# Weaving Fourier products into the inverses of a gated delta rule

## The chip, the cores and the metric

One core of a Trainium2 chip runs the whole program. The metric is the device time of one execution, in microseconds (us).

## The reference

Two model blocks follow each other on a sequence of 512 tokens of width 1024. The first has two layers with four kinds of attention and a gated feed-forward. The second, the tail here, adds a context of 256 tokens and mixes positions in two ways: a Fourier mix over four groups of 128 channels, and a gated delta rule in both directions over chunks of 64 tokens with four heads. Then come an output projection and a convolutional feed-forward.

```
def fourier_mix(u, w_f):
    ug = u.reshape(bsz, length, F_GROUPS, F_DIM)
    y = jnp.fft.fft2(ug, axes=(1, 3), norm='ortho').real
    return jnp.einsum('blgc,gcd->blgd', y, w_f)

def gated_delta_chunked(q, k, v, beta, g, s0):
    ...
    a_mat = jnp.where(strict, jnp.einsum('nbhid,nbhjd->nbhij', kb, kc) * decay, 0.0)
    t_inv = lax.linalg.triangular_solve(eye + a_mat, ...)
    u_val, w_key = t_inv @ vb, t_inv @ (kb * jnp.exp(gc)[..., None])
    ...
    def step(s, xs):
        v_new = u_i - w_i @ s
        o_i = qd_i @ s + a_i @ v_new
        s = s * jnp.exp(gl_i)[..., None, None] + kd_i^T @ v_new
        return s, o_i

y = concat(fourier_mix(u), rmsnorm(o_forward + o_backward) * silu(z)) @ w_out
```

## The kernel before

**Dense products.** A planner (`Dense`) writes out all projections as blocks in order and gives each output one of four PSUM banks (dense 0 and 1, scores 0 and 1) and each weight item its place in the stream. SP loads item n into raw slot n mod 4, once the last reader of item n - 4 has marked itself on `dense_mark`; GpSimd (POOL) loads the same item in rounded form into one of three high slots and subtracts the two (L2870), so TensorE (PE) runs three passes per block (L840 to L842).

**The tail up to the scan.** PE first computes the projections qkv, u and z. Then come two products that fold the Fourier weights into a cosine and a sine matrix (L1255). For each of the four Fourier groups follow eight channel products of 128 x 128 (L1264), whose result ScalarE (ACT) copies to p1 and p2, and eight position products of 128 x 512 (L1271) with a 2 MB position matrix, which accumulate in one bank and which ACT copies (L1867). The position matrix has a place of its own (`DFT_AT`); SP loads it in four loads (L820) during qkv. After the Fourier groups PE transposes v (L1283), makes the six row matrices of the decays (L1295, L1296) in dense 0 and 1, transposes k (L1303, L1311), and computes the token products of keys and queries (`token_products`, L1327).

**The inverses.** The twelve chunks are taken in three groups; each has both directions (d = 0, 1) of two token blocks. A triangular inverse is built in levels 1 to 5. In a level PE makes z from the masked matrix (`level_z`, L1354), ACT copies it (L1899), PE makes the update (`level_update`, L1366), and VectorE (DVE) subtracts it (L2643) and transposes (L2646), which the next level's z waits for. POOL makes each level's mask (L3044). In group 0 DVE also makes the other groups' matrices in each level (`make_a`, `make_x`, L2606 to L2627), and PE transposes four of them after levels 4 and 5 (`turn_x`, L1339). At the end of a group `w_and_u` forms w (L1380) and u (L1393), in the banks turned, scores and dense; ACT copies w and DVE copies u (L2661).

**The scan.** Its twelve steps are spread: four in group 1 (one after each z of levels 1 to 4), four in group 2, four behind. `scan_read` multiplies the state with w (L1413) and, from the fifth step on, with q (L1422); DVE subtracts (L2670), decays the state (L2678), and later adds (L2688); `scan_write` forms the update of the state (L1437) and the output (L1446), whose sum DVE makes (L2699). For the last steps POOL adds parts of the output (L3074), between which it splits the first weights of the output projection. All engines run their instructions in program order. Direction d writes the bank dense d or scores d, in the half of the partitions that its chunk has.

```
for lev in range(1, LEVELS):
    level_z(g, lev)
    if g and lev < LEVELS - 1:
        scan_read(4 * (g - 1) + lev - 1)
    level_update(g, lev)
    if g and lev < LEVELS - 1:
        scan_write(4 * (g - 1) + lev - 1)
    if g == 0 and lev >= LEVELS - 2:
        turn_x(...)
w_and_u(g)
```

Of the kernel before, what the change touches and what calls it, by code (L numbers as in the profile page):

```python
# [18 lines left out]
ALU = mybir.AluOpType  # L19
# [3 lines left out]
P = 128  # L23
D_MODEL, SEQ, DEPTH = 1024, 512, 2
KC = D_MODEL // P
TB = SEQ // P
# [111 lines left out]
THIRD_AND_FOURTH = {("qI", 0): 2, ("qI", 1): 3, ("up", 1, 0): 2, ("up", 1, 1): 3}  # L138
EARLY = [("ab", 1), ("qkv", 0, 1), ("qkv", 1, 1)]


class Dense:


    def __init__(self):
# [57 lines left out]
        for n, (key, k, total, item, m) in enumerate(rows):  # L203
            if key not in self.outs:
# [3 lines left out]
                if key[0] < TAIL:  # L208
                    b = THIRD_AND_FOURTH.get(key[1:], b)
                self.bank[key], self.turn[key] = b, used[b]  # L210
                used[b] += 1
            opens = item is not None and item not in self.items
# [97 lines left out]
AB = 16  # L310

# [40 lines left out]
DFT_AT, WF_AT = 82, 90  # L352
ROWSUM_AT, ROWBAR_AT, DECAY_AT, A_AT, AL_AT, T_AT = 8, 14, 84, 76, 82, 90
TT_AT, Z_AT, TTB_AT, TTG_AT, WT_AT, U_AT, KD_AT = 92, 94, 20, 35, 8, 12, 16
STATE_AT, O2_AT, OSCAN_AT, FOURIER_AT = 22, 56, 60, 20
# [8 lines left out]
def build_program(nc, x_in, stream, small_in, ada_in, cond_in, const_in, const2_in, dft_in, wf_in, ctx_in, out):  # L364
    with ExitStack() as ctx:
# [147 lines left out]
        dft = [flat(region(f"dft{n}", DFT_AT + 2 * n, 2)) for n in range(4)]  # L513
# [12 lines left out]
        wc, ws, p1, p2 = rows_of("fourier", FOURIER_AT, 4)  # L526
# [107 lines left out]
        CONST2_LANDED, DFT_LANDED = (16 * (n + ADA_N // 3) for n in (3, 6))  # L634
# [138 lines left out]
        def _(sp):  # L773
# [24 lines left out]
            for n, item in enumerate(DENSE.item_list):  # L798
# [36 lines left out]
        def _(pe):  # L835
# [421 lines left out]
            evac_wait((TAIL, "u", 3))  # L1257
            for g in range(4):
                for m in range(2):
                    b = custom("pc", g, m)  # L1260
                    if g == 0:
                        evac_wait((TAIL, "wf", m))
# [4 lines left out]
                b = custom("py", g)  # L1267
                for m in range(2):
                    evac_wait((TAIL, "pc", g, m))
                    for t in range(TB):  # L1270
                        last = nc.tensor.matmul(banks[b], (p1, p2)[m][:, t * P:(t + 1) * P],  # L1271
                                                dft[2 * m + t // 2][:, (t % 2) * SEQ:(t % 2 + 1) * SEQ],
                                                start=(m == 0 and t == 0), stop=(m == 1 and t == TB - 1))
                last.then_inc(dense_mark, 1)

            pe.wait_ge(l2_var, L2_VAR + 1)
            pe.wait_ge(ab_act, 6)
            pe.wait_ge(ab_step, 10)
            for t in range(XB):
# [5 lines left out]
                last.then_inc(v_turned, 1)  # L1285
            for d in range(2):
                for p in range(GROUPS):
# [5 lines left out]
                    else:  # L1293
                        evac_wait((TAIL, "py", 3 - k))
                    nc.tensor.matmul(dense[:, k % 2, :], chunk_ones, rowsum[k], start=True, stop=False)  # L1295
                    nc.tensor.matmul(dense[:, k % 2, :], ident, rowbar[k], start=False, stop=True  # L1296
                                     ).then_inc(row_ready, 1)
            for t in range(XB + 1):
# [19 lines left out]
            XT_BANK = (scores[:, 0, :], scores[:, 1, :], O[:], dense[:, 1, :])  # L1318
# [51 lines left out]
            def w_and_u(g):  # L1370
# [3 lines left out]
                for d in range(2):  # L1374
# [8 lines left out]
                    last.then_inc(w_ready, 1)  # L1383
                for j in range(2):
# [13 lines left out]
            def scan_read(s):  # L1398
# [10 lines left out]
                for h in range(GH):  # L1409
                    hc = slice(h * P, (h + 1) * P)  # L1410
                    for d in range(2):
                        c, hs = chunk_of(d, i)
                        last = nc.tensor.matmul(dense[hs, d, hc], wT[2 * d + c][:, c64(ORDER_GDN[d][n] % 2, h)],  # L1413
                                                state[d][:, hc], start=True, stop=True)
                last.then_inc(c_ws, 1)
                if latent_no(s) >= 0:
                    for h in range(GH):
                        hc = slice(h * P, (h + 1) * P)
                        for d in range(2):
                            c, hs = chunk_of(d, i)  # L1420
                            at = ORDER_GDN[d][n] * P + CHUNK * c
                            last = nc.tensor.matmul(scores[hs, d, hc], cv[:, h, at:at + CHUNK], state[d][:, hc],  # L1422
# [3 lines left out]
            def scan_write(s):  # L1426
# [13 lines left out]
                if latent_no(s) >= 0:  # L1440
                    for h in range(GH):
                        hc = slice(h * P, (h + 1) * P)
                        for d in range(2):
                            c, hs = chunk_of(d, i)
                            b = ORDER_GDN[d][n]
                            last = nc.tensor.matmul(dense[hs, d, hc], dec[mat_no(d, b // 2)][hs, c64(b % 2, h)],  # L1446
# [1876 lines left out]
```

## Time and profile before

| what | value |
|---|---|
| median of 3 runs | 2998.88 us (2996.25 to 3001.03) |
| the profiled execution | 2997.56 us |
| its span | 2995.7 us |
| PE busy (matmul) | 2908.3 us, 97% |
| DVE, ACT, POOL busy | 1550.1, 757.3, 1603.7 us |
| chain that ended last | PE 73%, issue 9%, POOL 8%, DVE 7%, DMA 1% |
| granted PE clock, mean | 0.99 |

The span is the time from the first to the last instruction in the profile; the execution's own time is 1.9 us longer. Busy time of PE is modelled, and two matmuls that follow each other overlap in it. A float32 matmul shows as two records ("x16" for eight matmuls). "Idle before" in a timeline row is the time in which the engine stood still ahead of it, with the instruction that ended the wait.

### The profile page before, as it was taken

What the parts mean: (1) busy time and instruction counts of PE and PEld (TensorE: products, weight loads), DVE (VectorE), ACT (ScalarE), POOL (GpSimd) and SP (SyncE); (2) the same over time, 40 slices, a digit from 0 to 9 for tenths busy, and PEclk for the clock granted to TensorE, in tenths of its full rate; (3) what the DMA queues carried; (4) which work ended last, traced back from release to release, by engine and by line L of the source; (5) the groups of instructions that cost most, each with busy time, mean ns of one, the idle gap of its engine ahead of it and who ended that gap; (6) DMA issues with size and microseconds to landing.
All of it is one profiled execution on the core that took longest, in us unless ns stands there. A gap on an engine that the chain in (4) does not pass through costs nothing.

```text
span 2995.7 us, 41055 instructions
## 1 busy us (share of the span) xinstructions
PE 2908.3 (97%) x16317; PEld 2315.4 (77%) x16317; DVE 1550.1 (52%) x2975; ACT 757.3 (25%) x1611; POOL 1603.7 (54%) x1117
## 2 busy tenths in 40 slices
PE   8999999999999999999999999999999987999997
PEld 5777777778888877777777788888787687788886
DVE  6663452357785146543423567861352377766611
ACT  4333331113111033343322122121131223311110
POOL 4344455556555653345556575556534254566664
PEclk9999999999999999999999999999999999999999
DMA  6444444446776544344444457765533000355553
GB/s 223 141 137 142 151 147 170 169 143 211 255 269 218 196 164 160 127 141 150 153 162 166 157 197 275 257 227 185 190 113 126 1 3 23 113 188 192 197 196 134
DMA packets 133566, 491.97 MB, mean 164 GB/s; under 512 B 14960, under 2 KB 14960, under 8 KB 132480
## 3 DMA queue, kind: packets, MB, share of 16 engines
q1 hardware_dynamic: 71024, 262.56, 26.2%
q0 software_dynamic: 60912, 221.80, 20.7%
q10 hardware_dynamic: 1440, 4.99, 0.4%
q8 instruction: 130, 2.13, 0.3%
q14 instruction: 60, 0.49, 0.1%
HBM read 487.16 MB, written 2.13 MB: 163 GB/s over the span
## 4 chain that ended last, share of the span: by engine, by line
PE 73%; issue 9%; POOL 8%; DVE 7%; DMA 1%; ACT 1%; POOLq 0%; DVEq 0%; ACTq 0%
PE dense L840 20%; PE dense L842 19%; PE dense L841 19%; POOL raw_lo L2870 5%; PE scores L840 2%; PE scores L842 2%; PE scores L841 2%; PE scores L1067 1%; DMA weights_hi<-stream 1%; PE O L1101 1%; PE O L1135 1%; POOL weights_hi L2855 1%; PE turned L1089 1%; PE dense L1271 1%; PE scores L1121 1%
## 5 line engine op out<-in xcount | busy, mean ns | idle before, releaser
L2870 POOL TENSOR_TENSOR raw_lo<-raw,weights_hi 128x1024 fp32r<-128x1024 f32 x422 | 1013.4, 2402 | 43.5 <-DMA weights_hi<-stream 34.1
L2855 POOL DMA_DIRECT2D weights_hi<-stream x423 | 245.0, 579 | 1123.5 <-PE dense L842 1033.9
L840 PE MATMUL dense<-h_hi,weights_hi 128*128 128x512 f32 x2096 | 835.3, 399 | 10.0 <-POOL raw_lo L2870 8.6
L842 PE MATMUL dense<-h_hi,raw_lo 128*128 128x512 f32 x2096 | 818.3, 390 | 0.0
L841 PE MATMUL dense<-h_lo,weights_hi 128*128 128x512 f32 x2096 | 817.0, 390 | 0.0
L840 PEld LDWEIGHTS dense<-h_hi,weights_hi 128*128 128x128 f32 x2096 | 393.9, 188 | 115.7 <-issue 28.1
L842 PEld LDWEIGHTS dense<-h_hi,raw_lo 128*128 128x128 f32 x2096 | 393.8, 188 | 85.0
L841 PEld LDWEIGHTS dense<-h_lo,weights_hi 128*128 128x128 f32 x2096 | 394.5, 188 | 76.9
L840 PE MATMUL dense<-hidden_hi,weights_hi 128*128 128x512 f32 x528 | 205.7, 390 | 1.9 <-POOL raw_lo L2870 1.9
L842 PE MATMUL dense<-hidden_hi,raw_lo 128*128 128x512 f32 x528 | 205.4, 389 | 0.0
L841 PE MATMUL dense<-hidden_lo,weights_hi 128*128 128x512 f32 x528 | 205.4, 389 | 0.0
L2831 DVE SCALAR_TENSOR_TENSOR side_b<-scores,small_sb,side_b 128x441 f32<-128x441 f32 (+2 forms) x176 | 122.3, 695 | 66.0 <-ACT side_b L1957 60.5
L2375 DVE SCALAR_TENSOR_TENSOR x<-dense,x 128x512 f32<-128x512 f32 x32 | 22.1, 691 | 233.1 <-PE dense L842 233.1
L2163 DVE TENSOR_TENSOR y_parts<-O,y_parts 128x512 fp32r<-128x512 f32 x24 | 16.6, 692 | 236.7 <-ACT y_parts L1667 236.7
L840 PEld LDWEIGHTS dense<-hidden_hi,weights_hi 128*128 128x128 f32 x528 | 99.1, 188 | 22.9 <-POOL raw_lo L2870 2.4
L842 PEld LDWEIGHTS dense<-hidden_hi,raw_lo 128*128 128x128 f32 x528 | 99.1, 188 | 20.6
L841 PEld LDWEIGHTS dense<-hidden_lo,weights_hi 128*128 128x128 f32 x528 | 99.1, 188 | 20.5
L840 PE MATMUL dense<-y_parts,weights_hi 128*128 128x512 f32 x256 | 103.4, 404 | 2.8 <-DVE y_parts L2275 2.8
L1693 ACT ACTIVATE probs<-probs,neg_max 128x128 f32<-128x128 f32 (+3 forms) x128 | 71.0, 556 | 134.9 <-DVE neg_max L2207 134.9
L1579 ACT ACTIVATE swapped<-dense 32x512 f32<-32x512 f32 x144 | 84.8, 589 | 79.6 <-PE dense L842 77.4
L3044 POOL TENSOR_TENSOR a_level<-gdn_a,const 128x512 f32<-128x512 f32 x36 | 48.5, 1361 | 100.3 <-DVE gdn_a L2612 55.3
L842 PE MATMUL dense<-y_parts,raw_lo 128*128 128x512 f32 x256 | 100.1, 391 | 0.0
(466 smaller groups left out, 4744.0 us busy)
## 6 DMA issues: line engine op xcount, KB each, us to landing
raw<-stream SPq DMA_DIRECT2D x423, 512.0 KB, 3.4
weights_hi<-stream POOLq DMA_DIRECT2D x423, 512.0 KB, 4.5
ada_w<-ada SPq DMA_DIRECT2D x48, 512.0 KB, 5.2
decays<-stream ACTq DMA_DIRECT2D x8, 512.0 KB, 4.4
gates<-f_scratch SPq DMA_DIRECT2D x2, 1536.0 KB, 9.6
x<-x_in SPq DMA_DIRECT2D x2, 1024.0 KB, 8.1
cond_rows<-cond SPq DMA_DIRECT2D x2, 1024.0 KB, 6.7
dft<-dft SPq DMA_DIRECT2D x4, 512.0 KB, 4.9
```

Of the source, the lines that this page charges most:

```text
L840: nc.tensor.matmul(to, wh, xh, start=first, stop=False)
L841: nc.tensor.matmul(to, wh, xl, start=False, stop=False)
L842: return nc.tensor.matmul(to, wl, xh, start=False, stop=final)
L1067: last = nc.tensor.matmul(scores[:, hh, 0:n], qT[c % 2][half, s * P:(s + 1) * P], keys[half, k0:k1], start=True, stop=True)
L1089: last = nc.tensor.transpose(turned[:, hh, m * P:(m + 1) * P], prob(i, hh, SEQ)[:, m * P:(m + 1) * P], ident)
L1101: last = nc.tensor.matmul(O[half, m * P:m * P + n], values[:, m, v0:v0 + HEAD_DIM], probT(hh, m, n), start=(m == 0), stop=True, skip_group ...
L1579: last = nc.scalar.activation(swapped[32 * q:32 * q + 32, :], src[32 * (q ^ 1):32 * (q ^ 1) + 32, :], ACT.Copy)
L1693: last = nc.scalar.activation(prob(s, hh, n), src, ACT.Exp, bias=neg_max[:, at:at + 1], scale=QK_SCALE if name == "D" else 1.0, accum_out= ...
L2831: nc.vector.scalar_tensor_tensor(out=u, in0=v, scalar=small[:, tap:tap + 1], in1=u, op0=ALU.mult, op1=ALU.add).then_inc(conv_step if m < 7 ...
L2855: nc.gpsimd.dma_start(w_hi(s), stream[DENSE.items[DENSE.weight_list[w]]]).then_inc(hi_landed[s], 16)
L2870: nc.gpsimd.tensor_tensor(lo, src, hi, ALU.subtract).then_inc(weights_lo, 1)
L3044: nc.gpsimd.tensor_tensor(by8(a_level[d]), by8(a_mat[mat_no(d, PAIR_GDN[d][g])]), level_mask(d, lev), ALU.mult).then_inc(t_masked, 1)
```

## The change

The position matrix becomes four items of the weight stream, between the last z item and the first item of the output projection, and so is loaded into the four raw slots; the raw loads of the first four items of the output projection wait until the last position product has read them. Of the Fourier groups only group 0 is computed ahead: its channel products where they were, its position products behind the transposes of v. The channel products of group 1 stand ahead of the token products, two of its position products behind them, and the other six behind the levels of inverse group 0. Fourier groups 2 and 3 lie in inverse groups 1 and 2: channel products behind level 1, two position products behind each of levels 2 to 5. Their copies and roundings on ACT and the remainders on POOL move along. The position sums lie in dense 1 (group 0: scores 0), so both directions of a scan step now share dense 0, and scores 0 for q. The state, whose place holds p1 and p2 for a while, is cleared after `w_and_u(0)`. The constants of the inverses (const2) are loaded ahead of the last matrix item.

```
+FOURIER_BANKS = {"wf": lambda r: r, "pc": lambda g, m: m if g < 2 else (1, 3)[m], "py": lambda g: (2, 1, 1, 1)[g]}
...
+            if key == (TAIL, "wf", 0):
+                for i in range(4):
+                    self.items[(TAIL, "dft", i)] = len(self.items)
...
+            if key == (TAIL, "py", 3):
+                for i in range(4):
+                    self.item_mark[(TAIL, "dft", i)] = marks
...
+FOUR_LOW_AT = ((1, 1), (1, 3), (2, 1))
+BEFORE_LEVELS, BY_LEVEL = 2, ((1, 2, 1, 1, 1), (0, 2, 2, 2, 2), (0, 2, 2, 2, 2))
...
-                    for i in range(4):
-                        sp.dma_start(dft[i], dft_in[i]).then_inc(s_dft, 16)
                     sp.dma_start(wf, wf_in).then_inc(s_dft, 16)
-                if item == (TAIL, "out2", 3):
+                if item == (TAIL, "dft", 2):
                     sp.wait_ge(dense_mark, DENSE.item_mark[(TAIL, "z", 3)])
                     sp.dma_start(const2, const2_in[:, SEQ:CONST2_N]).then_inc(s_const, 16)
...
+            def position_products(g, first, n):
+
+                if first == 0:
+                    custom("py", g)
+                for at in range(first, first + n):
+                    m, t = divmod(at, TB)
+                    if t == 0:
+                        evac_wait((TAIL, "pc", g, m))
+                    item = DENSE.items[(TAIL, "dft", at // 2)]
+                    if g == 0 and t % 2 == 0:
+                        pe.wait_ge(landed[item % RAW_SLOTS], 16 * (item // RAW_SLOTS + 1))
+                    last = nc.tensor.matmul(banks[DENSE.bank[(TAIL, "py", g)]], (p1, p2)[m][g][:, t * P:(t + 1) * P],
+                                            raw(item % RAW_SLOTS)[:, (t % 2) * SEQ:(t % 2 + 1) * SEQ],
+                                            start=(at == 0), stop=(at == 2 * TB - 1))
+                if first + n == 2 * TB:
+                    last.then_inc(dense_mark, 1)
...
+            channel_products(0)
             pe.wait_ge(l2_var, L2_VAR + 1)
...
+            position_products(0, 0, 2 * TB)
             for d in range(2):
                 for p in range(GROUPS):
...
                     last.then_inc(w_ready, 1)
+                evac_wait((TAIL, "py", g + 1))
                 for j in range(2):
...
-                        last = nc.tensor.matmul(dense[hs, d, hc], wT[2 * d + c][:, c64(ORDER_GDN[d][n] % 2, h)],
+                        last = nc.tensor.matmul(dense[hs, 0, hc], wT[2 * d + c][:, c64(ORDER_GDN[d][n] % 2, h)],
                                                 state[d][:, hc], start=True, stop=True)
...
             pe.wait_ge(decay_done, 2 * GROUPS)
+            channel_products(1)
             token_products(2, 4, KK_BANK[2], kk_ready)
...
             token_products(0, 0, QK_BANK[0], qk_ready)
+            evac_wait((TAIL, "pc", 1, 0))
             token_products(1, 0, QK_BANK[1], qk_ready)
+            position_products(1, 0, BEFORE_LEVELS)
...
                     if g and lev < LEVELS - 1:
                         scan_write(4 * (g - 1) + lev - 1)
+                    if g and lev == 1:
+                        channel_products(g + 1)
+                    if BY_LEVEL[g][lev - 1]:
+                        position_products(g + 1, (0 if g else BEFORE_LEVELS) + sum(BY_LEVEL[g][:lev - 1]), BY_LEVEL[g][lev - 1])
                     if g == 0 and lev >= LEVELS - 2:
                         turn_x(2 * (lev - LEVELS + 2))
...
+                    if g and lev == 2:
+                        act.wait_ge(t_masked, level_no(0, LEVELS - 1, 1))
+                        copy_channels(g + 1)
                     for d in range(2):
                         act.wait_ge(t_z, turn_no(g, lev, d))
                         nc.scalar.activation(z_mat[d], turned[:, d, :], ACT.Copy).then_inc(t_zc, 1)
...
+                copy_positions(g + 1)
+                round_positions(g + 1)
                 for d in range(2):
                     act.wait_ge(w_ready, 2 * g + d + 1)
...
                 w_and_u(g)
+                if g == 0:
+                    clear_states()
...
             for w in range(W_OUT, W_OUT + 3):
                 issue(w)
+            four_low(3)
             add_output(8, kd_ready, 2 * UNITS)
```

## Rows read from the trace of the kernel before

**Rows 1.** Stretches, first and last chunk group: us, busy per engine, PEclk, DMA share
```profile
2366.20:2416.40 50.20, 42.89 (x1056) 41.48 (x1057) 39.68 (x52) 12.60 (x22) 29.49 (x21) 0.86 0.01 3
2464.40:2514.80 50.40, 44.69 (x1024) 42.41 (x1025) 37.28 (x56) 17.12 (x46) 20.60 (x19) 0.97 0.04 9
```

**Rows 2.** Timeline of PE, the Fourier groups: start, us, then the instructions
```profile
2318.40 2.01 PE L1264 MATMUL dense<-fourier,y_tail 128*128 128x128 f32 x16
2320.24 7.09 PE L1271 MATMUL dense<-dft,fourier 128*128 128x512 f32 x16
...
2344.72 1.04 PE L1283 MATMUL turned<-const,cv 128*128 128x128 f32 x8
```

**Rows 3.** Timeline of PE, levels of group 0
```profile
2373.07 3.58 PE L1354 MATMUL turned<-tt_mat,a_level 64*64 64x64 f32 x64 [2.01 <-POOL a_level L3044]
...
2379.26 1.15 PE L1354 MATMUL turned<-tt_mat,a_level 64*64 64x64 f32 x32 [0.69 <-DVE t_mat L2646]
...
2381.53 2.06 PE L1366 MATMUL turned<-z_mat,t_mat 64*64 64x64 f32 x64
2385.37 1.15 PE L1354 MATMUL turned<-tt_mat,a_level 64*64 64x64 f32 x32 [1.78 <-DVE t_mat L2646]
...
2395.99 2.06 PE L1339 MATMUL scores<-const,gdn_decay 64*64 64x64 f32 x64
```

**Rows 4.** Timeline of DVE, level 2 of group 0
```profile
2380.36 2.33 DVE L2606 TENSOR_TENSOR gdn_a<-gdn_decay,const 128x512 f32<-128x512 f32 x2
...
2383.81 0.67 DVE L2643 TENSOR_TENSOR tt_mat<-tt_mat,turned 128x512 f32<-128x512 f32 x1
```

**Rows 5.** Timeline of PE, levels 2 and 3 of group 1
```profile
2424.76 3.47 PE L1354 MATMUL turned<-tt_mat,a_level 64*64 64x64 f32 x64 [2.12 <-DVE t_mat L2646]
...
2433.46 1.15 PE L1354 MATMUL turned<-tt_mat,a_level 64*64 64x64 f32 x32 [1.10 <-DVE t_mat L2646]
...
2435.95 1.09 PE L1413 MATMUL dense<-state,wT 128*64 128x128 f32 x16
```

**Rows 6.** Timeline of PE in group 2, and a row of PE's waits there
```profile
2464.46 2.93 PE L1354 MATMUL turned<-tt_mat,a_level 64*64 64x64 f32 x64 [2.59 <-DVE u_rows L2661]
...
2473.95 2.03 PE L1354 MATMUL turned<-tt_mat,a_level 64*64 64x64 f32 x64
2477.31 1.09 PE L1413 MATMUL dense<-state,wT 128*64 128x128 f32 x16 [1.33 <-DVE o L2699]
...
2501.65 2.03 PE L1354 MATMUL turned<-tt_mat,a_level 64*64 64x64 f32 x64
...
PE turned L1380 <- POOL tt_gain L3060: 1.0, 1, 1.0
```

**Rows 7.** SP's timeline, the chain, PE's timeline; the page's DMA issues (us to landing)
```profile
2154.28 1.75 SPq L820 DMA_DIRECT2D dft<-dft  x4
...
2158.85 7.03 DMA weights_hi<-stream
...
2168.84 0.47 PE L840 MATMUL dense<-hx_hi,weights_hi 128*128 128x512 f32 x1 [2.14 <-POOL raw_lo L2870]
...
raw<-stream SPq DMA_DIRECT2D x423, 512.0 KB, 3.4
weights_hi<-stream POOLq DMA_DIRECT2D x423, 512.0 KB, 4.5
```

**Rows 8.** Timeline of POOL, the last scan steps
```profile
2518.18 3.01 POOL L3074 TENSOR_TENSOR o<-o,oscan 64x512 f32<-64x512 f32 x2 [4.17 <-ACT oscan L1891]
2521.27 4.66 POOL L2870 TENSOR_TENSOR raw_lo<-raw,weights_hi 128x1024 fp32r<-128x1024 f32 x2
```

**Rows 9.** Stretches with their clock: w and u of groups 0 and 1; two low ones
```profile
2404.80:2415.60 10.80, 10.69 (x128) 10.33 (x128) 6.83 (x9) 2.17 (x4) 9.33 (x7) 0.68 0.01 2
2454.40:2461.90 7.50, 7.43 (x128) 7.12 (x128) 6.26 (x7) 2.17 (x4) 7.50 (x6) 1.00 0.01 3
...
2373.20:2376.60 3.40, 3.40 (x68) 3.40 (x69) 0.00 (x0) 0.60 (x1) 2.30 (x2) 0.51 0.02 5
...
2424.40:2427.80 3.40, 3.04 (x57) 3.07 (x59) 2.67 (x5) 0.60 (x1) 0.98 (x1) 0.51 0.00 0
```

More of the change, by code:

```diff
@@ L310 @@
 AB = 16
+FOUR_LOW_AT = ((1, 1), (1, 3), (2, 1))
+BEFORE_LEVELS, BY_LEVEL = 2, ((1, 2, 1, 1, 1), (0, 2, 2, 2, 2), (0, 2, 2, 2, 2))
+assert all(sum(b) + (0 if g else BEFORE_LEVELS) == 2 * TB for g, b in enumerate(BY_LEVEL))
 SMALL = {}
@@ L1256, in _, with channel_products @@
                                  start=True, stop=True).then_inc(dense_mark, 1)
[L1257 to L1258 removed]
+            def channel_products(g):
                 for m in range(2):
                     b = custom("pc", g, m)
[L1261 to L1262 removed]
                     for t in range(TB):
@@ L1266, in _ @@
                     last.then_inc(dense_mark, 1)
[L1267 to L1274, printed above, removed]
+            def position_products(g, first, n):
[13 more added lines that the diff above has]
+                    last.then_inc(dense_mark, 1)
+            evac_wait((TAIL, "u", 3))
+            for m in range(2):
+                evac_wait((TAIL, "wf", m))
+            channel_products(0)
             pe.wait_ge(l2_var, L2_VAR + 1)
@@ L1421, in scan_read @@
                             at = ORDER_GDN[d][n] * P + CHUNK * c
-                            last = nc.tensor.matmul(scores[hs, d, hc], cv[:, h, at:at + CHUNK], state[d][:, hc],
+                            last = nc.tensor.matmul(scores[hs, 0, hc], cv[:, h, at:at + CHUNK], state[d][:, hc],
                                                     start=True, stop=True)
@@ L1445, in scan_write @@
                             b = ORDER_GDN[d][n]
-                            last = nc.tensor.matmul(dense[hs, d, hc], dec[mat_no(d, b // 2)][hs, c64(b % 2, h)],
+                            last = nc.tensor.matmul(dense[hs, 0, hc], dec[mat_no(d, b // 2)][hs, c64(b % 2, h)],
                                                     u_rows[2 * d + b % 2][hs, hc], start=True, stop=True)
@@ L1863, in _, with copy_channels, copy_positions, round_positions @@
                 nc.scalar.activation((wc, ws)[r], src, ACT.Copy, scale=FFT_SCALE).then_inc(done, 1)
-            for g in range(4):
-                for key, dst in ((("pc", g, 0), p1), (("pc", g, 1), p2), (("py", g), yT[:, g, :])):
-                    src, done = result((TAIL,) + key)
-                    nc.scalar.activation(dst, src, ACT.Copy).then_inc(done, 1)
+            def copy_channels(g):
+                for m in range(2):
+                    src, done = result((TAIL, "pc", g, m))
+                    nc.scalar.activation((p1, p2)[m][g], src, ACT.Copy).then_inc(done, 1)
+            def copy_positions(g):
+                src, done = result((TAIL, "py", g))
+                nc.scalar.activation(yT[:, g, :], src, ACT.Copy).then_inc(done, 1)
+            def round_positions(g):
+                act.wait_ge(evacuated[bank_of((TAIL, "py", g))], evac_count((TAIL, "py", g)))
+                nc.scalar.activation(four_hi[:, g, :], yT[:, g, :], ACT.Copy).then_inc(four_rounded, 1)
+            copy_channels(0)
             act.wait_ge(ab_step, 10)
@@ L2593, in _, with clear_states @@
                                         ).then_inc(k_scaled, 1)
-            evac_wait((TAIL, "py", 3))
-            for d in range(2):
-                nc.vector.memset(state[d], 0.0).then_inc(ab_step, 1)
-            dve.wait_ge(ab_step, 14)
+            dve.wait_ge(ab_step, 12)
+            def clear_states():
+                evac_wait((TAIL, "py", 1))
+                for d in range(2):
+                    nc.vector.memset(state[d], 0.0).then_inc(ab_step, 1)
+                dve.wait_ge(ab_step, 14)
             KK_BANK = {2: scores[:, 0, :], 0: scores[:, 1, :], 1: O[:]}
```

43 lines of the change are left out of this document (24 added, 19 removed).

## The prediction

> **What bounds the kernel now.** I read the page first: TensorE (PE) is busy for 97% of the span and heads the chain that ended last, so a microsecond taken out of its path counts in full. The change touches one stage of the tail, the gated delta rule, so I next cut that stage by time. While the inverses and the scan run, PE is less full: 42.9 of 50.2 us in the first of the three chunk groups, 44.7 of 50.4 in the last [rows 1]; it waits for VectorE and GpSimd between the levels of an inverse. Ahead of it, PE computes the four Fourier groups back to back: the channel products of one group take 1.84 us, three groups take 2344.72 - 2318.40 = 26.3 us, so a group costs 8.77 us and one of its eight position matmuls (8.77 - 1.84) / 8 = 0.87 us [rows 2]. The question is how much of 26.3 us fits into the waits. For that I went through the timeline level by level.
>
> **What is removed.** Three groups leave the stretch before the v transposes: **-26.3 us**, all on the path. What the scan's preparation needs is ready early enough: the row matmuls start some 26 us sooner, near 2322, and their rowbar operands, on VectorE, follow a 480 KB load that SP issues at z3's end in both kernels, ahead of the fourth matrix load now; that last load is wanted by the seventh position matmul only, over 7 us after its issue (channel products 1.8, six position matmuls 5.2, the v transposes between), against 3.4 for such a load [rows 7]. I take nothing for it.
>
> **What comes back, group 0 of the inverses.** (a) The channel products of Fourier group 1 stand between the last key copy and the first token product, on which VectorE waits: **+1.8**. (b) Two position matmuls (1.74) before level 1 lie in a 2.01 us wait for GpSimd's mask [rows 3]: 0. (c) After level 1, one (0.87) in a gap of 0.69: +0.2. After level 2, two (1.74) in a gap of 1.78: 0 [rows 3]. Group 0 is paced by VectorE: its next subtraction comes at 2383.81, right behind make_a's work begun at 2380.36 [rows 4], while the update's first half ends near 2382.6, so about 1.2 us of lateness on PE is absorbed; one matmul after level 3 costs 0. (d) After levels 4 and 5 turn_x follows the update without a gap [rows 3], and w_and_u waits for its copies: one matmul each, +0.9 and +0.9. Together **+2.0**. The copy and the rounding of group 1 on ScalarE, and the two memsets of the state on VectorE, are operations of 512 columns, for which I take VectorE's 0.67 each [rows 4]: 1.3 and 1.3. The first pair falls under the w products' first half, ahead of the w copies; the second under level 1's z products (2.0). Nothing for them; without those covers they would cost just that.
>
> **Group 1.** After level 1 comes a channel block (1.84) in a gap of 2.12; then two matmuls (1.74) in gaps of 1.1 to 1.3; behind the gap z's two halves stand apart (from 2433.46 to the read at 2435.95 is 2.5 us for 1.9 of work) and can close up [rows 5]. The first half starts late, the second hardly: 0 to 0.3 a level, **+0.4** in all. The matmuls after level 5 delay w and u by 0.8, but the copies of u wait for VectorE there: in the group behind, z waits for them, not for PE [rows 6]. ScalarE's two channel copies stand ahead of level 2's z copy; their products are done before z is, so 0.
>
> **Group 2.** Here PE's work and VectorE's chain are nearly equal. z runs before the scan's read, and the read then waits only 1.33 for VectorE's output sums [rows 6]. 1.84 after level 1, 1.74 after levels 2 and 3, with about 0.1 for the change of tile shape: +0.6 three times. Level 5's z follows level 4 without a gap [rows 6], so +1.9 there; after level 5 the wait for tt_gain is 1.0 [rows 6], so +0.75. Together **+4.4**, on the path to the last four scan steps.
>
> **Loads.** The four 512 KB loads of the matrix leave the queue at 2154.28. The weights issued at 2158.85 took 7.03 us to land, against a median of 4.5 over all 423, and PE stood 2.14 us behind them [rows 7]. With 2 MB less ahead, that stall goes: **-2.1** (bounds 0 and -2.1). In exchange the raw loads of the first four w_out items wait for the last position matmul, in old time near 2507 (2501.65 plus z, update and two matmuls) [rows 6]. GpSimd wants the first at 2521.27, behind output sums for which it idles 4.17 us [rows 8]; four loads at 3.4 us each, even one after another, need 13.6 us for all. Cost 0, upper bound one load, 3.4. The added rounding remainder (1.3 us) sits in the same 4.17 us idle.
>
> **One bank for both directions.** No row shows a scan product in that form. Nearest is z (two row tiles and two column tiles on the two halves of one bank): 64 passes of 64 columns in 2.06 us, about 1.87 without the tail of the last pass [rows 3, 6]. The full array takes 16 passes of 128 columns in 1.84 [rows 2], 0.115 each, thus 0.057 per 64 columns; 0.029 is half. So tiles overlap inside a bank, and I take 0. The scan's products have that pace across two banks: 16 passes of 128 columns in 1.09, last pass included, about 0.93 without it [rows 5]. The upper bound is no overlap: 0.93 more in each of 28 blocks (12 reads of w, 8 of q, 8 output products), 26 us. The Trainium skill, TensorEngine Tiling (Array Packing), Gotcha 1, says that different row tiles cannot access the same PSUM bank simultaneously. The output products are row tiles, so by it 8 x 0.93 = 7.4 us would come back. The z rows of this trace, with row tiles on different partitions of one bank, speak against it; the reads are column tiles only.
>
> Sum so far: -26.3 + 1.8 + 2.0 + 0.4 + 4.4 - 2.1 = **-19.8**.
>
> **The clock.** In this stage PE's granted clock falls from 2.4 to 1.2 GHz in places, each after PE had been idle part of the time. At 2373.2, after the 2.01 us wait, z took 3.58 instead of 2.03: 1.5 lost. At 2424.4, after the 2.12 us wait, 3.47: 1.2 lost beyond the usual gaps. In group 0's w and u the clock averaged 0.68, and the block took 10.8 us where group 1's took 7.5 at full clock: about 3.0 lost [rows 3, 5, 9]. The change fills just the first two waits with full-array products, and the gaps before the third. I count the first two back, and half the third, since no wait stands directly before it: **-4.2**. Bounds: 0, and -6.6 if all of the third goes and a low stretch at the head of group 2 too, where z took 2.93 instead of 2.03 [rows 6]; but the 2.6 us wait before that one stays uncovered.
>
> Total -24.0. The profiled execution took 2997.56 us, 1.3 below the median of the runs: 2973.6 for such an execution, **2975 us** as a median. A difference under 0.2% (6 us) is about what measuring this kernel can't tell from none.
>
> **Rivals.** (1) **The clock doesn't come back.** Low stretches merely move; for it: group 2 keeps z at 2.03 with PE gaps of 1.3 us, while group 0's w and u run low behind smaller ones, so idleness alone doesn't explain them. -19.8: 2979 us. (2) **The inserted products cost double.** PE runs in program order, so whatever wakes a chain late repeats in each level: ScalarE copies ahead of z's, VectorE slack that I overrate. 8.6 us once more: 2984 us (with the clock's gain). Against it: ScalarE is 25 and 34% busy here [rows 1]. (3) **The shared bank makes the two directions run in turn.** Place: scan_read and scan_write, where VectorE waits for each product. Price 26 us for all 28 blocks; above 0.71 us per block it eats the 19.8. Without the clock's gain +6.2, 3005 us, slower; with it +2, 3001. Against: the rows of z. (4) **Fewer waits usable than seen**, the DMA stall staying as well: it only shifts within the range.
>
> **How the numbers follow.** Forecast (2970 to 2978) 0.60; rival 1 0.20; rival 2 0.13; rival 3 0.05, over half of it beyond 0.2%; remainder 0.02 near no change. The range runs from 2969 (all of the clock's 6.6 back and group 2 cheaper by 3) to 2984 (rival 2); it leaves out rival 3 and the tails, no more than 2 in 10. Faster 0.93, same 0.04, slower 0.03.
>
> **What would show it.** Right: one Fourier group before the row matmuls; first z product some 26 us earlier than 2373; z in group 0 waiting well under 1 us; group 2's levels about 0.6 us longer than now; w_out starting about 24 us earlier; no 2.14 us stall near 2168; scan products still about 1.09 us per 16 passes; clock 1.0 around level 1 of groups 0 and 1. Wrong: scan products of 1.9 us; PE waiting for ScalarE before z's update; GpSimd waiting for raw at w_out; a clock share in the three groups as low as 0.86 again.

## The result, and the profile of the changed kernel

The changed kernel takes 2977.69 us (median of 4 runs, 2973.11 to 2982.55); the kernel before, beside it, 2997.57 us (4 runs). The ratio is 0.993, 95% interval 0.9918 to 0.9943: 20 us faster. The forecast was 2975.

The page of the changed kernel, busy time and the chain that ended last:

```profile
PE 2905.6 (98%) x16317; PEld 2306.7 (78%) x16317; DVE 1549.1 (52%) x2975; ACT 758.1 (25%) x1611; POOL 1606.5 (54%) x1117
...
PE 74%; issue 9%; POOL 9%; DVE 5%; DMA 2%; ACT 1%; POOLq 0%; DVEq 0%; ACTq 0%
```

PE has nearly the same work (2908.3 us before) in a shorter span; VectorE's share of the chain fell from 7% to 5%. Of the 19.7 us by which the span is shorter, 2.7 is busy time of PE; the rest is time in which PE waited.

Stretches of the changed kernel, with the columns of [rows 1, 9]: group 0 from its first z to its first w product, w and u of group 0, groups 1 and 2 up to the next group's or step's start, and the last four scan steps up to the output projection.

```profile
2351.72:2383.77 32.05, 30.28 (x780) 25.14 (x780) 26.76 (x37) 8.93 (x16) 17.17 (x12) 1.00 0.01 3
2383.77:2392.09 8.32, 7.43 (x129) 7.15 (x129) 7.19 (x9) 3.24 (x6) 8.09 (x7) 1.00 0.01 2
2392.09:2440.08 47.99, 45.86 (x929) 38.54 (x929) 37.70 (x54) 10.56 (x18) 24.91 (x20) 1.00 0.01 3
2440.08:2494.11 54.03, 53.15 (x1057) 45.29 (x1057) 38.19 (x56) 19.57 (x50) 23.20 (x21) 1.00 0.15 51
2494.11:2530.84 36.73, 23.85 (x280) 19.53 (x281) 27.31 (x41) 12.57 (x38) 22.32 (x13) 0.93 0.09 30
```

Group 2 now keeps PE busy for 53.15 of 54.03 us, where 44.69 of 50.40 stood in [rows 1]; the first z product starts at 2351.72 and not at 2373.07; the granted clock is 1.00 in all three groups, while [rows 9] had 0.68 in w and u of group 0.

The timeline of PE in the changed kernel: the head of the stage, level 1 of group 0 with its product behind, the head of group 2 with its channel products and the next read, and the reads of scan steps 9 to 11.

```profile
2310.62 1.12 PE L1266 MATMUL dense<-wf 128*128 128x512 f32 x2 [0.97 <-DVE y_tail L2620]
2312.64 1.13 PE L1274 MATMUL dense<-fourier_cos,y_tail 128*128 128x128 f32 x8 [0.89 <-ACT fourier_sin L1894]
...
2351.72 2.37 PE L1377 MATMUL turned<-tt_mat,a_level 64*64 64x64 f32 x64
2353.92 2.03 PE L1389 MATMUL turned<-z_mat,t_mat 64*64 64x64 f32 x64
2355.89 1.12 PE L1289 MATMUL dense<-raw,p 128*128 128x512 f32 x2
...
2440.08 2.08 PE L1377 MATMUL turned<-tt_mat,a_level 64*64 64x64 f32 x64 [1.72 <-DVE u_rows L2717]
...
2448.11 1.16 PE L1274 MATMUL dense<-fourier_cos,y_tail 128*128 128x128 f32 x8
2449.11 1.06 PE L1274 MATMUL scores<-fourier_sin,y_tail 128*128 128x128 f32 x8
2450.09 2.08 PE L1377 MATMUL turned<-tt_mat,a_level 64*64 64x64 f32 x64
2452.21 1.09 PE L1437 MATMUL dense<-state,wT 128*64 128x128 f32 x16
...
2501.37 1.47 PE L1437 MATMUL dense<-state,wT 128*64 128x128 f32 x16 [2.49 <-DVE o L2755]
...
2509.78 1.09 PE L1437 MATMUL dense<-state,wT 128*64 128x128 f32 x16 [2.71 <-DVE o L2755]
...
2517.05 1.09 PE L1437 MATMUL dense<-state,wT 128*64 128x128 f32 x16 [2.49 <-DVE o L2755]
```

The 2.01 us ahead of level 1 are gone and z no longer takes 3.58 [rows 3]. The reads in group 2 wait for nothing, where they waited 1.33 [rows 6]. The scan products, both directions in one bank, still take 1.09 us at full clock (1.47 in one row of the last steps, where the granted clock is 0.93 on average). The second row is a wait that I had not predicted: `channel_products(0)` now stands behind the copies of both Fourier weights, where the first half needed only the first copy. And the last scan steps keep three waits of 2.5 to 2.7 us that nothing fills.

At the loads, the timeline of POOL in the changed kernel has, at the place where PE stood 2.14 us before [rows 7]:

```profile
2166.09 2.39 POOL L2928 TENSOR_TENSOR raw_lo<-raw,weights_hi 128x1024 fp32r<-128x1024 f32 x1 [1.26 <-DMA weights_hi<-stream]
```

POOL still waits for a load, but PE no longer for POOL.

**Where the 19.7 us of the two spans lie.** I call "stage" the time from the first wf product to the first output projection. It went from 245.58 us (2306.69 to 2552.27) to 222.21 (2308.63 to 2530.84): -23.4. The stall at the loads: -2.3. The rest, some +6, lies outside what was changed: +2.6 in the first 92 us and +1.6 at 2273, each with one more stretch at 1.2 GHz, and 1.7 in small pieces behind the stage. Such differences come and go between runs of one program (a second trace of the kernel before reaches the stage at 2310.75 and not at 2306.69), which is why the experiments below are compared by stage and by ratio.

### The profile page after: what moved, and what is told of

It reads as the page before. It is cut to its first block, busy times and chain, and to the rows that moved or that the text cites. A ratio compares the mean times of both kernels' runs of the same rounds, so it can differ in the third digit from the quotient of the medians.

```text
span 2976.0 us, 41064 instructions
## 1 busy us (share of the span) xinstructions
PE 2905.6 (98%) x16317; PEld 2306.7 (78%) x16317; DVE 1549.1 (52%) x2975; ACT 758.1 (25%) x1611; POOL 1606.5 (54%) x1117
## 4 chain that ended last, share of the span: by engine, by line
PE 74%; issue 9%; POOL 9%; DVE 5%; DMA 2%; ACT 1%; POOLq 0%; DVEq 0%; ACTq 0%
PE dense L851 20%; PE dense L853 19%; PE dense L852 19%; POOL raw_lo L2928 6%; PE scores L851 2%; PE scores L853 2%; PE scores L852 2%; DMA weights_hi<-stream 1%; PE scores L1078 1%; PE O L1112 1%; PE O L1146 1%; POOL weights_hi L2913 1%; PE turned L1100 1%; PE scores L1132 1%; PE turned L1377 1%
## 5 line engine op out<-in xcount | busy, mean ns | idle before, releaser
L851 PE MATMUL dense<-y_parts,weights_hi 128*128 128x512 f32 x256 | 103.5, 404 | 2.8 <-DVE y_parts L2327 2.8
L852 PE MATMUL dense<-y_parts,weights_hi 128*128 128x512 f32 x256 | 99.9, 390 | 0.0
```

Of the source, the lines that this page charges most:

```text
L851: nc.tensor.matmul(to, wh, xh, start=first, stop=False)
L852: nc.tensor.matmul(to, wh, xl, start=False, stop=False)
```

## Experiments

Stretches of all traced kernels, worked out from the starts of the same instructions in each timeline (us); in brackets the mean granted clock of the stretch where it is under 1.00. "Tokens" is the start of the token products behind the first wf product.

| kernel | tokens | group 0 | its w, u | group 1 | group 2 | last steps | stage |
|---|---|---|---|---|---|---|---|
| before | 59.49 | 31.78 (0.89) | 11.58 (0.71) | 48.03 (0.96) | 50.34 (0.97) | 37.47 (0.91) | 245.58 |
| b1_before | 59.49 | 31.62 (0.95) | 8.45 | 48.10 (0.96) | 49.64 | 36.29 (0.91) | 240.49 |
| x3_loads | 59.49 | 32.02 (0.89) | 8.43 | 47.05 | 50.12 (0.97) | 37.81 (0.95) | 241.81 |
| x4_one_bank | 59.48 | 31.19 (0.95) | 8.43 | 49.97 (0.90) | 49.65 | 37.81 (0.95) | 243.43 |
| x1_ahead | 60.60 | 31.81 (0.89) | 11.58 (0.71) | 48.08 (0.96) | 50.35 (0.97) | 37.45 (0.91) | 246.77 |
| x5_filler | 60.57 | 30.81 | 11.58 (0.71) | 47.20 | 49.64 | 36.43 (0.91) | 243.13 |
| x2_twice | 62.57 | 32.05 | 11.58 (0.71) | 48.00 | 54.03 | 37.86 (0.86) | 253.00 |
| after | 36.17 | 32.05 | 8.32 | 47.99 | 54.03 | 36.73 (0.93) | 222.21 |
| e0_after | 36.15 | 32.05 | 8.32 | 48.00 | 54.03 | 37.60 (0.95) | 223.06 |
| s1_shift2 | 37.86 | 32.06 | 8.31 | 48.00 | 54.03 | 36.11 (0.95) | 223.28 |
| x7_later | 35.13 | 32.06 | 8.31 | 48.00 | 52.89 (0.94) | 38.21 | 221.49 |
| x8_better | 33.01 | 32.05 | 8.32 | 47.99 | 49.64 | 36.43 (0.99) | 214.34 |

**The first theory.** From the first pair of traces alone I read: insertions cost 11 to 12 us, not 8.6, and the clock gave back about 8, not 4.2. The first four runs test that.

**e0_after**: the changed kernel, unedited.

> The changed kernel again, on the chip of the next three. Every theory: 0.9934 of the kernel before (2978 us), and the delta-rule stage (from the first wf product to the first output projection) 222.2 us, against 245.6 in the kernel before. Theory A, which the first pair of traces suggests: 26.3 us of products left the path, some 11 to 12 us came back where they were inserted, and the clock gave back about 8, not the 4.2 that was predicted; so no stretch at 1.2 GHz inside the three chunk groups here either.

Measured: 2976.18 us, ratio 0.9927 (0.9915 to 0.9939). The groups last what they did, to 0.01 us; the stage, 223.06, is 0.85 longer, which lies in the last scan steps.

**x1_ahead**: all four groups ahead again, everything else as changed.

```
+            for g in range(4):
+                channel_products(g)
+                position_products(g, 0, 2 * TB)
...
-                    if BY_LEVEL[g][lev - 1]:
-                        position_products(g + 1, ...)
```

> The changed kernel with its weaving alone undone: all four Fourier groups stand ahead of the v transposes again; the matrix in the weights' slots, the single bank of the scan and the places of the roundings stay. Theory A (the weaving is the whole gain in the stage, the bank and the loads give none there): stage 245.6 plus 0.9 for the wait for both wf copies, near 246.5; stretches at 1.2 GHz back in the three groups; whole kernel 0.9985 to 1.000 of the kernel before, the missing stall of 2.2 us left as the difference. Rival B (the shared bank or the roundings, moved off group 0, bring a part): stage clearly under 245, by as much as they bring.

Measured: 2996.70 us, ratio 1.0001 (0.9992 to 1.0009), at the upper edge of what was expected; stage 246.77. Every stretch of the groups is within 0.05 us of the kernel before, at the same clocks. The weaving is the whole gain of the stage: bank, places of the roundings and of the matrix bring nothing there, and rival B falls. Tokens start 1.1 us later than before, which is the wf wait.

**x2_twice**: x1_ahead, and the products of three groups once more at the woven places (there as groups 4 to 6).

```
+        for g in range(7):
...
+                        position_products(g + 4, ...)
```

> The kernel of x1_ahead, with the products of three Fourier groups computed a second time at the woven places (their results are thrown away, the used ones are those computed ahead). Against x1_ahead this is the net cost of the insertion alone, with nothing removed. Theory A (insertion 11.4, clock back 8, or the stage's -23.4 = -26.3 + net): stage 2.9 to 3.5 us longer than x1_ahead's, with no stretch at 1.2 GHz in the three groups. Prediction's sizes (8.6 inserted, 4.2 of clock back): 4.4 longer. Rival C (the clock comes back because 26 us less full-array work stand ahead, not because gaps are filled): stretches at 1.2 GHz stay, stage about 11 longer.

Measured: 3004.41 us, ratio 1.0022 (1.0013 to 1.0031); the stage is 6.2 us longer than in x1_ahead, 2.0 of it at the tokens and 3.7 in group 2. My first theory (2.9 to 3.5) fell, and the prediction's sizes (4.4) came out nearer; they count 1.5 us of clock for w and u of group 0, which did not come back here, and without it they give 5.9. Rival C falls for the levels and seems to hold for one place, as the stretches of x2_twice show (the columns are those of [rows 1]):

```profile
2376.66:2408.71 32.05, 30.28 (x780) 25.14 (x780) 26.76 (x37) 8.93 (x16) 17.17 (x12) 1.00 0.02 4
2408.71:2420.29 11.58, 10.69 (x128) 10.36 (x129) 7.18 (x9) 3.13 (x6) 8.08 (x7) 0.71 0.00 1
2420.29:2468.29 48.00, 45.86 (x928) 38.55 (x929) 37.70 (x54) 10.45 (x18) 24.92 (x20) 1.00 0.01 3
2468.29:2522.32 54.03, 53.15 (x1057) 45.30 (x1057) 38.19 (x56) 19.46 (x50) 23.19 (x21) 1.00 0.14 48
```

Three stretches equal those of the changed kernel to 0.01 us. In w and u, PE runs the same instructions behind the same 32 us, and yet 3.3 us longer, at 0.71.

**x5_filler**: x1_ahead, and short bf16 products in the waits.

```
+            idle_products(dense[:, 1, :], 8)
...
+                    idle_products(dense[:, 1, :], FILLERS[g][lev - 1])
```

> The kernel of x1_ahead, with short bf16 products of the identity (384 columns, 0.17 us each, thrown away) in the waits of the inverses: 8 before the levels, 4, 8, 4, 2, 2 in group 0, 10, 5, 5, 5, 4 in group 1, 5, 5, 5, 0, 4 in group 2. They fit into the waits and so cost next to nothing by themselves. Theory A (activity in the gaps keeps the clock at 2.4 GHz, worth about 8 us): stage 5 to 8 us shorter than x1_ahead's, low stretches gone, whole kernel 0.997 to 0.998 of x1_ahead. Prediction's size: 4 shorter. Rival C (the clock doesn't follow the gaps): no difference, or longer by up to 2 us for the products that don't fit.

Measured: 2993.20 us, ratio 0.9985 (0.9976 to 0.9994), against 1.0001 of x1_ahead; the intervals overlap by 0.0002. The stage is 3.6 us shorter, 2.6 of it in the three groups and 1.0 in the last scan steps, where no filler stands. Its first three stretches:

```profile
2374.48:2405.29 30.81, 28.39 (x788) 24.96 (x788) 26.74 (x37) 8.93 (x16) 16.81 (x12) 1.00 0.01 4
2405.29:2416.87 11.58, 10.69 (x128) 10.36 (x129) 7.17 (x9) 2.64 (x5) 8.70 (x7) 0.71 0.01 1
2416.87:2464.07 47.20, 42.53 (x925) 36.87 (x926) 37.77 (x54) 8.66 (x15) 24.46 (x20) 1.00 0.01 3
```

So PE kept busy in the waits holds the clock in the levels (-1.0, -0.9 and -0.7 in the three groups), with no useful work moved; the 2.6 is what the prediction counted for the levels (2.7), not the 5 to 8 that I now expected. In w and u of group 0 it does nothing.

**The second theory.** Insertions cost what was predicted, and two clock effects were mixed: one that filled waits remove, and one in w and u that falls where it will. The next runs test that, and the two terms still open.

**x3_loads**: the kernel before, its matrix loads spread.

```
-                    for i in range(4):
-                        sp.dma_start(dft[i], dft_in[i]).then_inc(s_dft, 16)
...
+                if item[:2] == (TAIL, "qkv") and item[2] in (5, 7, 9, 11):
+                    sp.dma_start(dft[(item[2] - 5) // 2], ...).then_inc(s_dft, 16)
```

> The kernel before, with the four 512 KB loads of the position matrix issued one at a time, behind the fifth, seventh, ninth and eleventh qkv weights, and no longer all four in a row behind the second. Theory A (the row of 2 MB holds up the next weights): the wait of 2.14 us for weights near 2170 goes, the kernel is 2.1 us faster, 0.9993 of the kernel before. Rival (the stall only moves to the spread loads, or lies under something else): a stall of similar size elsewhere, ratio 1.000.

Measured: 2996.32 us beside 2998.32, ratio 0.9991 (0.9983 to 1.0). That is the predicted size, but the interval reaches 1.0, so the time alone can't tell 2 us from none; the trace can. The list of PE's waits between 2150 and 2290 is empty, with the same 2 MB issued in that stretch, where both traces of the kernel before have a wait of 2.1 us: the four loads in a row were the cause, not the 2 MB as such.

**x4_one_bank**: the kernel before, both directions in bank 0.

```
-   matmul(dense[hs, d, hc], wT[...   matmul(scores[hs, d, hc], cv[...   matmul(dense[hs, d, hc], dec[...
+   matmul(dense[hs, 0, hc], wT[...   matmul(scores[hs, 0, hc], cv[...   matmul(dense[hs, 0, hc], dec[...
```

> The kernel before with one edit of the change alone: both directions of a scan step in one bank, for the w products, the q products and the output products. The prediction: no cost, 16 passes stay at 1.09 us, ratio 1.000. Rival (the directions run in turn): 0.93 for each of 28 blocks, +26 us, ratio 1.009. Second rival, by the Trainium skill, TensorEngine Tiling (Array Packing), Gotcha 1 (row tiles of one bank run in turn): the 8 output-product blocks alone, +7.4 us, ratio 1.0025.

Measured: 2997.66 us, ratio 0.9997 (0.9988 to 1.0006), which excludes 7.4 us and 26. A w read, a q read and an output product of a step, timeline of PE in x4_one_bank:

```profile
2479.31 1.09 PE L1413 MATMUL dense<-state,wT 128*64 128x128 f32 x16 [1.33 <-DVE o L2699]
2480.21 1.07 PE L1422 MATMUL scores<-state,cv 128*64 128x128 f32 x16
...
2484.31 1.09 PE L1446 MATMUL dense<-u_rows,gdn_decay 64*64 64x128 f32 x16
```

The kernel before has the same durations across two banks: 1.09 for the w read [rows 5], 1.07 for the q read at 2478.21, and for the output product

```profile
2482.31 1.09 PE L1446 MATMUL dense<-u_rows,gdn_decay 64*64 64x128 f32 x16
```

The output product (64*64) has row tiles, the case of the Trainium skill, TensorEngine Tiling (Array Packing), Gotcha 1; here the row tiles write different partitions of the bank, and the measurement doesn't bear the rule out for that.

**b1_before**: the kernel before, unedited, for a second trace.

> The kernel before, unedited, for a second trace of one and the same program. In the runs so far the instructions of the chunk groups were the same in the kernel before, x1_ahead, x3_loads and x4_one_bank, but the stretches at 1.2 GHz lay elsewhere: from the first wf product to the read of scan step 8 took 208.1 in the first two and 204.0 and 205.6 in the others. Theory D (where the stretches fall differs from run to run, in one program too): 204 to 208.2 here, and the low stretches not all where the first trace has them. Theory E (they are fixed by the instructions): 208.1 again, with low stretches at 66.6, 80.2, 100.7, 117.8 and 158.7 us behind the first wf product.

Measured: 2998.23 us (one execution). The same stretches of one and the same program:

```profile
2377.14:2408.76 31.62, 26.01 (x768) 24.86 (x768) 26.33 (x37) 10.44 (x18) 16.37 (x12) 0.95 0.01 3
2408.76:2417.21 8.45, 7.43 (x128) 7.15 (x129) 7.07 (x9) 2.17 (x4) 8.45 (x7) 1.00 0.01 2
2417.21:2465.31 48.10, 38.65 (x896) 35.90 (x897) 36.81 (x52) 8.15 (x14) 28.27 (x22) 0.96 0.01 3
```

8.45 at full clock, where the first trace has 11.58 at 0.71. Theory D holds: the slow w and u is not fixed by the instructions. The four traces whose stage has the code of before (before, b1_before, x3_loads, x4_one_bank) range from 240.49 to 245.58; the first, on which the prediction rests, is the slowest.

**s1_shift2**: the changed kernel, two thrown-away position products ahead.

```
+                    if g == 0 and at == 0:
+                        for _ in range(2):
+                            nc.tensor.matmul(banks[...], p1[g][:, 0:P], raw(...)[:, 0:SEQ], start=True, stop=True)
```

> The changed kernel with two more position products (0.87 us each, thrown away) ahead of those of group 0. Open question: in x1_ahead, x5_filler and x2_twice the w and u products of the first chunk group run at 1.2 GHz (11.6 us from the first w product to the next group's z), in the changed kernel not (8.3), although x2_twice has the very same instructions from the row products to there. Theory D (the place in time decides, a matter of a microsecond or two): a shift by 1.75 us can bring the slow stretch back, block 11.6 us. Theory E (what stands tens of microseconds ahead decides: two or three groups' worth of full-array products in a row): no stretch at 1.2 GHz there, block 8.3 us, kernel 1.7 us slower than the changed kernel.

Measured: 2979.16 us, ratio 0.9936 (0.9923 to 0.9948); w and u 8.31. The shift brought no slow stretch back. With b1_before this refutes E as the whole story, too, since the kernel before has those products ahead and ran at full clock; but why the changed kernel and its relatives never show it in group 0 (5 traces) stays open. The time since the kernel's start doesn't decide it: w and u of group 0 begin at 2408.71 in x2_twice, slow, and at 2408.76 in b1_before, fast. Nor is the chip excluded for the kernels with all groups ahead: x1_ahead, x5_filler and x2_twice, all slow there, ran on one chip, and b1_before, x3_loads and x4_one_bank, all fast there, on two others (the chip of the first trace isn't on record). The chip alone isn't the cause either: e0_after, fast there, ran on the first.

**x7_later**: the better version, first attempt: group 3's position products in the waits of the last scan steps, and the channel products of group 0 behind the copy of their own half again.

```
+IN_STEPS = (3, 3, 2, 0)
...
+                    position_products(3, sum(IN_STEPS[:n]), IN_STEPS[n])
...
+                if n >= RAW_SLOTS and freed[:2] == (TAIL, "dft") and freed[2] < 3:
+                    sp.wait_ge(c_ws, (STEPS - 2, STEPS - 1, STEPS - 1)[freed[2]])
```

> The changed kernel with two edits: (1) the channel products of Fourier group 0 wait for the copy of their own half of the weights again, not for both (0.9 us of wait back); (2) the eight position products of group 3 leave the third chunk group, where x2_twice against x5_filler shows 4.4 us for group 3's products, and stand behind the writes of scan steps 8, 9 and 10 (3, 3, 2 of them), where the changed kernel's PE waits 2.49, 2.71 and 2.50 us for VectorE's output sums; the loads of w_out's first items follow the scan steps. Theory A: third chunk group 54.0 to about 50.9 us (the channel products stay), scan steps 8 to 11 unchanged to +0.6, wf wait -0.9: about 3.5 us faster than the changed kernel, ratio 0.9915 against the kernel before. Rival (the loads or the remainders of w_out come late and PE waits for them behind the stage; or the copy of group 3 holds up the scan's last output): gain eaten by a wait near the first output projection.

Measured: 2973.07 us, ratio 0.9916 (0.9902 to 0.9929). Timeline of x7_later: PE behind the write of step 8, then GpSimd, VectorE's second output scale, and PE's wait for it:

```profile
2493.08 2.84 PE L1295 MATMUL dense<-raw,p 128*128 128x512 f32 x6
2495.86 1.09 PE L1442 MATMUL dense<-state,wT 128*64 128x128 f32 x16
...
2522.64 2.33 POOL L2939 TENSOR_TENSOR raw_lo<-raw,weights_hi 128x1024 fp32r<-128x1024 f32 x1
2522.69 3.43 DVE L2800 TENSOR_TENSOR o<-o,const 128x512 f32<-128x512 f32 x2 [0.45 <-POOL const L3154]
...
2525.57 1.26 PE L1516 MATMUL scores<-const,o 128*128 128x128 f32 x8 [4.04 <-DVE o L2800]
```

The products fit (reads of steps 9 and 10 follow them without a gap), but two things took part back. The first is a low stretch: group 2 lasts 52.89 and not the expected 50.9. Its last part, from the first w product to the read of step 8, in x7_later and, with the same instructions of PE, in x8_better (below):

```profile
2476.86:2488.38 11.52, 10.68 (x128) 10.35 (x129) 4.71 (x6) 2.17 (x4) 7.47 (x8) 0.70 0.40 132
2475.07:2483.34 8.27, 7.43 (x128) 7.15 (x129) 4.71 (x6) 2.17 (x4) 7.48 (x8) 1.00 0.16 36
```

So the slow w and u can fall in group 2 as well, and in a kernel with woven groups; less these 3.25 us, group 2 takes 49.64 although a whole channel block stands in it. The second is a relative of the rival: GpSimd's remainder for w_out moved beside the output scale, whose two instructions take 3.43 us there and 1.29 in the changed kernel, and PE waits 4.04. They end at 2526.12, which is 1.15 behind the end of GpSimd's subtraction (2524.97): nearly all of their 1.29 us of work lies behind it. The Trainium skill, SBUF — State Buffer, "SBUF: two separate sides", says the same: of a VectorE operation with two SBUF inputs and a GpSimd operation that reads SBUF, the later one is blocked for the whole of the other. The trace agrees within 0.14 us.

The last steps are 1.5 us longer than in the changed kernel, so by stage x7_later gains only 0.7; its ratio matches the expected 0.9915, but the interval overlaps the changed kernel's.

**x8_better**: x7_later and four edits.

```
+            pool.wait_ge(gated_lo, GATED_LO + 4)
             low(W_OUT + 2)
...
+                if g == 1:
+                    channel_products(3, (0,))
...
+            channel_products(1)
             pe.wait_ge(kh_stored, XB)
...
-"wf": lambda r: r
+"wf": lambda r: 3 * r
```

> The kernel of x7_later with four more edits, each for a wait that its trace shows: (1) GpSimd makes the remainder of w_out's third item only after the last gated outputs are split, since VectorE's output scale took 3.43 us beside it where the changed kernel has 1.29: -2.1; (2) half of group 3's channel products stands behind w and u of the second chunk group, where PE waits 1.7 us for the copies of u: -0.7; (3) group 1's channel products stand ahead of the wait for the last turned keys (0.68): -0.7; (4) the second weight product of the Fourier transform gets a bank of the scan, and no longer waits 0.95 for VectorE's gate: -0.9. Theory A: 4.4 us less than x7_later, ratio 0.990 against the kernel before. Rival: ScalarE's copies, which now come at other places, take part of it back; 1 to 3 us less.

Measured: 2968.24 us (2965.31 to 2971.49), ratio 0.9901 (0.9884 to 0.9917): faster than both kernels, 9 us under the changed one. It is 4.8 under x7_later (4.4 expected), with four runs each too few to tell 4.8 from none. The second output scale, from VectorE's timeline:

```profile
2517.66 1.29 DVE L2802 TENSOR_TENSOR o<-o,const 128x512 f32<-128x512 f32 x2 [0.45 <-POOL const L3156]
```

And the stretch of group 2:

```profile
2433.70:2483.34 49.64, 44.37 (x1032) 41.83 (x1033) 38.14 (x56) 18.32 (x48) 21.86 (x20) 1.00 0.04 9
```

49.64 us is what group 2 takes at full clock with nothing inserted (b1_before), although half of a channel block is still in it. By stage x8_better is 7.2 us under x7_later: 2.1 ahead of the token products, where edits 3 and 4 are (1.6 expected), 1.8 in the last steps, where edit 1 is (2.1 expected), and 3.25 in group 2, which is the low stretch that isn't there this time. Edit 2 brought nothing: less that stretch, group 2 is as long in x7_later.

## Why the prediction was right

**The removal (-26.3)** was right, less 1.0: the row products start at 16.53 us behind the first wf product where it was 41.83 (-25.3). I had read the channel products as staying "where they were" and missed that their wait now covers both copies. That is the one step of the sum that was missing. Of the signs named for being right, the first z product "some 26 us" earlier came out at 21.4: less by this 1.0, and by the 4.2 us at 1.2 GHz ahead of the stage.

**The insertions (predicted +8.6)** held, the sum to 0.2 and each term to 0.8, once each is taken at full clock. Token products: tokens minus rows 19.64 against 17.66, +2.0 (predicted 1.8). Group 0: 32.05 against 30.81 in x5_filler, +1.2, and more if the fillers cost something themselves (predicted 2.0). x5_filler is the comparison since no trace with bare waits has full clock there. Group 1: 48.00 against 47.05 in x3_loads, +0.95 (0.4). Group 2: 54.03 against 49.64 in b1_before, +4.4 (4.4). w and u: -0.1. Sum 8.4; that it is so near 8.6 is partly luck, since group 0 came out 0.8 lower and group 1 0.55 higher. Rival 2, double costs, is out.

**The clock (predicted -4.2, bounds 0 to -6.6).** The mechanism was right in the levels: with products in the waits, x5_filler, x2_twice and all five traces with the changed groups 0 and 1 have clock 1.00 there, and the five traces with bare waits do not (0.89 to 0.96, group 1 once 1.00). The third term, half of group 0's w and u, was mis-read: in the pair of traces all 3.3 us came back, but not because waits were filled, since x2_twice fills them and keeps the low stretch, and b1_before leaves them and has none. Taken together, from the first z product to the read of scan step 8, full clock is 30.81 + 8.44 + 47.05 + 49.64 = 135.9; the four traces of before's stage have 141.7, 137.8, 137.6 and 139.2. So the clock was worth 5.8 in the profiled pair and 3.2 on average. The forecast lay between them, in part by luck: the levels, counted at 2.7, gave 2.6 in the pair and 2.4 on average, but w and u, counted at 1.5, gave 3.1 and 0.8, from a stretch that comes and goes. Rival 1 was right in its argument, that idleness alone doesn't explain that stretch, and wrong in its result, since the clock of the levels came back.

**The loads (-2.1)** held: in x3_loads, with nothing else changed, the 2.1 us wait is gone. **The bank (0)** held by x4_one_bank; rival 3 is out. Costing the delayed w_out loads at nothing held too: the first product of the output projection follows at 2530.84 without a wait for a load, and the list of GpSimd's work has none before its remainders for w_out.

**Sum.** Stage, averaged: 222.6 (two traces) against 242.8 (four), -20.2; by the terms -25.3 + 8.4 - 3.2 = -20.1. With the loads -22.3; the ratios 0.993 and 0.9927 give -21 and -21.9, within their intervals. The -24.0 of the prediction was large by the missed 1.0 and by 1.0 of clock, the latter because the one profiled execution had more low stretches than most.

Of the signs named as wrong beforehand none appeared: no scan product of 1.9 us, no update waiting for ScalarE, no GpSimd wait for raw at w_out, no clock under 1.00 in the three groups (in x7_later relatives of two did: GpSimd's work beside VectorE, and 0.94 in group 2).

**Open.** Why w and u of group 0 run at 0.71 in some executions and at 1.00 in others; a shift of 1.75 us was tried, others were not, and no program is known to have been traced twice on one chip. Edits 3 and 4 of x8_better weren't separated from each other.

## What to carry to other kernels

Count the waits of an in-order engine one by one against the product that is to stand in them: the sums that came out of single gaps held to under 1 us per group, and the group where PE was already close to the recurrence (group 2) paid half of the whole price, so look for emptier stages behind it before weaving there. When a block is moved, read the waits that stand in front of it in its new place, and ask what the work moved aside will run next to. Take a clock term from more than one trace of the same program, since one trace can be off by several microseconds.

## What the runs showed of the hardware

Two executions of one program (before and b1_before) differ by 5.1 us in the stage, 3.8 of it in stretches at 1.2 GHz that only one of them has: group 0's w and u took 11.58 us or 8.45, group 2 took 50.34 or 49.64. Group 2's w and u took 11.52 or 8.27 for the same instructions in two woven kernels (x7_later and x8_better). With bare waits between bursts of small tiles, group 0's levels ran at a mean clock of 0.89 to 0.95 in all five traces; short bf16 products thrown away, in the same waits, kept it at 1.00 and made the three groups of a kernel with more instructions 2.6 us shorter (x5_filler against x1_ahead). A full channel block (1.84 us) inside group 2 cost nothing where no position products followed it (x7_later, less its low stretch). And two VectorE instructions of 128x512 took 3.43 us when a GpSimd subtraction of 128x1024 had begun just ahead of them, and 1.29 alone.
